# Up and down products of a gated MLP by seven half-block products each, with the samples apart and the gated values through DRAM

## The reference

```python
D_MODEL = 1024; SEQ = 1024; DEC_BATCH = 8; DEC_SEQ = 4; D_FF = 2816; FFN_CONV = 3
x = x + concat(heads) @ w_out                    # 1024 -> 1024
h = rmsnorm(x, ffn_norm_g)
up = h @ w_up                                    # 1024 -> 2 x 2816 (gate | value)
up, new_ffn = causal_dwconv(up, state, ffn_conv_w, ffn_conv_b)   # width 3, per column
gate, value = split(up)
y = x + (silu(gate) * value) @ w_down            # 2816 -> 1024
```

## Time and profile before

| what | value |
| --- | --- |
| median of 3 runs | 1661.88 us (1655.47 to 1668.57) |
| span of the profiled execution | 1659.6 us |
| TensorE busy | 1562.1 us, 94% |
| weight loads busy | 1477.7 us, 89% |
| VectorE busy | 996.4 us, 60% |
| ScalarE busy | 523.2 us, 32% |
| GpSimd busy | 307.1 us, 19% |
| bytes moved | 113.57 MB |

### The profile page before, as it was taken

One profiled execution on the slowest core, in us unless ns is written; L12 is line 12 of the kernel. 1 busy time (PEld: TensorE's weight loads), 2 busy tenths in 40 slices (PEclk: granted clock), 3 DMA queues, 4 the chain that ended last, 5 costly groups with the idle time before them and its releaser, 6 DMA issues.

```text
span 1659.6 us, 29004 instructions
## 1 busy us (share of the span) xinstructions
PE 1562.1 (94%) x11165; PEld 1477.7 (89%) x11165; DVE 996.4 (60%) x1507; ACT 523.2 (32%) x828; POOL 307.1 (19%) x698
## 2 busy tenths in 40 slices
PE   7999999997788888788999999999999999999998
PEld 7999999897577776455999999999999999999997
DVE  7444399786566666466445655646555565555654
ACT  6443333332344343444223221212212122121223
POOL 4000166563422342350000000000000000000000
PEclk8999999998799999899999999999999999999999
DMA  6211111222113110566212211102111021110104
GB/s 228 91 38 51 41 40 39 86 93 89 37 36 96 48 38 23 171 246 220 59 41 77 64 50 39 51 25 63 41 48 51 25 63 32 56 51 25 51 1 114
DMA packets 146857, 113.57 MB, mean 68 GB/s; under 512 B 21563, under 2 KB 134733, under 8 KB 145094
## 3 DMA queue, kind: packets, MB, share of 16 engines
q1 hardware_dynamic: 142456, 102.97, 21.0%
q0 software_dynamic: 1664, 6.29, 1.0%
q10 hardware_dynamic: 2656, 3.21, 0.5%
HBM read 90.59 MB, written 21.74 MB: 68 GB/s over the span
## 4 chain that ended last, share of the span: by engine, by line
PE 52%; DVE 1%; ACT 0%; DMA 0%; issue 0%; SPq 0%; DVEq 0%
PE f_up L3065 30%; PE f_down L3072 15%; PE f_up L193 4%; PE f_up L3025 1%; PE f_up L3052 1%; PE f_up L3072 0%; PE f_up L3110 0%; DMA f_rows<-in_ffn_conv_b 0%; PE f_up L3099 0%; PE f_down L3014 0%; ACT f_tail_tok L2827 0%; DVE dn_lo L2990 0%; PE f_down L3046 0%; DVE feat L2859 0%; DVE h_lo L2872 0%
## 5 line engine op out<-in xcount | busy, mean ns | idle before, releaser
L3065 PE MATMUL f_up<-h_hi,w_hi 128*128 128x352 f32 x1032 | 334.9, 324 | 0.0
L3065 PE MATMUL f_up<-h_hi,w_lo 128*128 128x352 f32 x1032 | 333.4, 323 | 0.0
L3065 PE MATMUL f_up<-h_lo,w_hi 128*128 128x352 f32 x1032 | 333.4, 323 | 0.0
L193 PE MATMUL proj<-x_hi,win_hi 128*128 128x352 f32 x672 | 219.9, 327 | 0.0
L193 PE MATMUL proj<-x_hi,win_lo 128*128 128x352 f32 x672 | 217.1, 323 | 0.0
L193 PE MATMUL proj<-x_lo,win_hi 128*128 128x352 f32 x672 | 216.9, 323 | 0.0
L3065 PEld LDWEIGHTS f_up<-h_hi,w_lo 128*128 128x128 f32 x1032 | 194.1, 188 | 0.0
L3065 PEld LDWEIGHTS f_up<-h_hi,w_hi 128*128 128x128 f32 x1032 | 193.8, 188 | 0.0
L3065 PEld LDWEIGHTS f_up<-h_lo,w_hi 128*128 128x128 f32 x1032 | 193.8, 188 | 0.0
L2949 DVE TENSOR_TENSOR feat<-f_down,feat 128x352 f32<-128x352 f32 x256 | 127.5, 522 | 65.2 <-PE f_down L3072 65.2
L3072 PE MATMUL f_down<-f_g_hi,dn_hi 128*128 128x352 f32 x512 | 165.3, 323 | 0.0
(11 more groups left out here) (464 smaller groups left out, 2799.4 us busy)
## 6 DMA issues: line engine op xcount, KB each, us to landing
w_raw<-in_w_up SPq DMA_DIRECT2D x44, 512.0 KB, 3.8
win_raw<-in_w_in SPq DMA_DIRECT2D x28, 512.0 KB, 4.1
dn_raw<-in_w_down SPq DMA_DIRECT2D x11, 1024.0 KB, 5.2
p_key<-in_cache_k SPq DMA_DIRECT2D x32, 256.0 KB, 3.6
x_scratch<-feat SPq DMA_DIRECT2D x1, 4224.0 KB, 12.0
feat<-x_scratch SPq DMA_DIRECT2D x8, 528.0 KB, 7.0
feat<-in_x_prompt SPq DMA_DIRECT2D x8, 512.0 KB, 8.0
c_DD<-dd_scratch SPq DMA_DIRECT2D x8, 512.0 KB, 4.0
```

What stands on the lines that cost most here:

```text
L193: mm = nc.tensor.matmul(out, w[:, k, :], x[:, k, g * TG:(g + 1) * TG], start=(k == 0 and i == 0), stop=(k == KT - 1 and i == 2))
L3065: mm = nc.tensor.matmul(up[u % RING][:, 0:TG], a[s][:, kk, :], b, start=(kk + x == 0), stop=(kk == KT - 1 and x == 2))
```

## The change

The samples leave the 1056 columns, so that the prompt is a square of two halves of 512 tokens. The up product of a pair (gate tile and value tile, 2 x 128 features, against 2 x 512 of the model's features and 2 x 512 tokens) is a 2 x 2 block product, made with seven products and fifteen sums instead of eight products. The names are P1 to P7. P1 to P4 and P6 have weights A11, A12, S4, A22 and S2, P5 and P7 have S1 and S3 (`W_OF`). The four weight sums S1 to S4 (`weight_sums`) are GpSimd's, 128x512 each, in each pair. The operand's sums are made once, before the first pair, and lie in SBUF with their high and low halves for all 22 pairs. A product is 4 x 3 matmuls of 512 columns, so a pair has 84. P1 is left in its bank and P2 is added on top of it, P7 and P4 on top of P6, P3 on top of P5; in between, copies are kept (`keep_u1` on ScalarE, the other six on VectorE), and the last of them write `f_pre`. The scaling by the root, which was part of L2915, is GpSimd's for three of the four quarters (`scale`). The high half of each weight tile is a ScalarE copy of 128x512 (`up_high`), the low half VectorE's (`up_low`), in a ring of five.

The gated values (1024 tokens) go to DRAM (`g_scratch`), and so does the residual (`h_scratch`). When all pairs are through, the down product runs in chunks of 3, 4 and 4 units of 256 features, by the same seven products: here each unit needs three token sums, three feature sums and two second ones on GpSimd (in chunk 0 the token sums are VectorE's), a high and a low half of both operands for each product (`b_high`, `b_low`), and results are added to `dn_C` in SBUF (`b_keep`). The residual comes back in chunk 1 (`add_h`). The 32 sample columns have products of their own on TensorE in plain fp32, in four column strips at a time: `few_up` (8 matmuls of 256 columns), `few_fold` (2) and `few_down` (4) for each pair.

```diff
+    h_scratch = nc.dram_tensor("h_scratch", (P, KT, SEQ), F32, kind="Internal").ap()
+    g_scratch = nc.dram_tensor("g_scratch", (FT, P, SEQ), F32, kind="Internal").ap()
...
+    OF = {"P1": PX, "P2": PX, "P6": PY, "P7": PY, "P4": PY, "P5": PZ, "P3": PZ}
+    FIRST_IN = ("P1", "P6", "P5")
+    LAST_IN = ("P2", "P4", "P3")
+    ORDER = ["P1", "P6", "P2", "P7", "P5", "P4", "P3"]
+    ORDER0 = ["P1", "P5", "P6", "P2", "P7", "P4", "P3"]
...
+    A11, A12, A21, A22 = quad(0, 0), quad(0, 1), quad(1, 0), quad(1, 1)
+    S1, S2, S3, S4 = (sums[:, s, :, :] for s in range(4))
+    W_OF = {"P1": A11, "P2": A12, "P3": S4, "P4": A22, "P5": S1, "P6": S2, "P7": S3}
+    S_NTH = {"P7": 1, "P6": 2, "P5": 3, "P3": 4}
...
+    CHUNKS = [(0, 3), (3, 4), (7, 4)]
...
+            def load_up(p):
+                if p == 0:
+                    sp.wait_ge(split_lo, done(NO - 1))
+                else:
+                    sp.wait_ge(sums_made, 4 * p)
+                    sp.wait_ge(up_lo, turn(p - 1, "P4") + 1)
+                    sp.wait_ge(few_done, p)
+                for s in range(2):
+                    sp.dma_start(up_raw[:, s, :, :], w_u[:, :, p * P + s * FF:(p + 1) * P + s * FF]).then_inc(up_in, 16)
...
+            def weight_sums(p):
+                pool.wait_ge(up_in, 32 * (p + 1))
+                if p == 0:
+                    pool.wait_ge(unit_done, FIRST - NG)
+                else:
+                    pool.wait_ge(up_lo, NP * p)
+                nc.gpsimd.tensor_tensor(S3, A11, A21, sub).then_inc(sums_made, 1)
+                pool.wait_ge(sums_made, 4 * p + 1)
+                nc.gpsimd.tensor_tensor(S2, A22, S3, sub).then_inc(sums_made, 1)
+                pool.wait_ge(sums_made, 4 * p + 2)
+                nc.gpsimd.tensor_tensor(S1, A21, A22, add).then_inc(sums_made, 1)
...
+            def scale(p, s, half, nth, count):
+                pool.wait_ge(kept, count)
+                if p == 0:
+                    pool.wait_ge(rstd_put, 3)
+                x = pre[s][:, F_PAD + half * HT:F_PAD + (half + 1) * HT]
+                nc.gpsimd.tensor_tensor(x, x, rstd[:, half * HT:(half + 1) * HT], mult).then_inc(scaled, 1)
...
+            for p in range(FT):
+                if p:
+                    scale(p - 1, 0, 1, 3, 6 * p)
+                    keep_tail(p - 1, 0)
+                put_state(p, 1)
+                put_state(p, 0)
+                if p + 1 < FT:
+                    weight_sums(p + 1)
+                scale(p, 1, 1, 1, 6 * p + 4)
+                scale(p, 1, 0, 2, 6 * p + 5)
+                keep_tail(p, 1)
+            scale(FT - 1, 0, 1, 3, 6 * FT)
...
+            def token_sums(k, u):
...
+                pool.wait_ge(b_lo, seq(k - 1, "P5", CHUNKS[k - 1][1] - 1) + 1)
+                nc.gpsimd.tensor_tensor(n["e"][1][:, u, :], n["d"][1][:, u, :], n["g"][1][:, u, :], sub).then_inc(b_t, 1)
+                pool.wait_ge(b_t, 3 * q + 1)
+                nc.gpsimd.tensor_tensor(n["g"][1][:, u, :], n["g"][1][:, u, :], n["a"][1][:, u, :], sub).then_inc(b_t, 1)
+                pool.wait_ge(b_t, 3 * q + 2)
+                pool.wait_ge(b_lo, seq(k, "P1", u) + 1)
+                nc.gpsimd.tensor_tensor(n["a"][1][:, u, :], n["e"][1][:, u, :], n["a"][1][:, u, :], add).then_inc(b_t, 1)
...
+            def feature_sums(k, u):
...
+                    pool.wait_ge(multiplied, NP * FT)
+                nc.gpsimd.tensor_tensor(n["e"][0][:, u, :], n["a"][0][:, u, :], n["g"][0][:, u, :], sub).then_inc(b_s, 1)
+                pool.wait_ge(b_s, 3 * q + 1)
+                pool.wait_ge(b_lo, seq(k, "P1", u) + 1)
+                nc.gpsimd.tensor_tensor(n["a"][0][:, u, :], n["d"][0][:, u, :], n["e"][0][:, u, :], sub).then_inc(b_s, 1)
...
+            def second_sums(k, u):
...
+                nc.gpsimd.tensor_tensor(n["b"][0][:, u, :], n["b"][0][:, u, :], n["a"][0][:, u, :], sub).then_inc(b_s4, 1)
+                pool.wait_ge(b_t, 3 * q + 3)
+                nc.gpsimd.tensor_tensor(n["b"][1][:, u, :], n["b"][1][:, u, :], n["a"][1][:, u, :], sub).then_inc(b_t4, 1)
...
+            def up_high(s):
...
+                else:
+                    act.wait_ge(multiplied, s - WR + 1)
...
+            def keep_u2(p):
+                dve.wait_ge(multiplied, turn(p, "P6") + 1)
+                dve.wait_ge(u1_kept, p + 1)
+                if p:
+                    dve.wait_ge(kept, 6 * p)
...
+            def keep_12(p):
+                dve.wait_ge(multiplied, turn(p, "P3") + 1)
+                dve.wait_ge(kept, 6 * p + 5)
+                plus(p, 6, part(0, 1), PZ[:, :], u2[:, :])
...
-            def add(it, d, bank):
-                dve.wait_ge(partial, ND * it + (d + 1))
-                h = hT[:, d // NG, (d % NG) * TG:(d % NG + 1) * TG]
-                nc.vector.tensor_tensor(h, bank[:, 0:TG], h, ALU.add).then_inc(summed, 1)
...
+            def b_low(k, name, u):
+                r = seq(k, name, u)
+                dve.wait_ge(b_hi, r + 1)
+                w, g = b_operands(k, name)
+                nc.vector.tensor_tensor(bw[r % RING_B][1][:, 0, :], w[:, u, :], r32(bw[r % RING_B][0][:, 0, :]), sub)
+                nc.vector.tensor_tensor(bg[r % RING_B][1][:, 0, :], g[:, u, :], r32(bg[r % RING_B][0][:, 0, :]), sub).then_inc(b_lo, 1)
...
+            def b_keep(k, name, f):
...
+                if name == "P1":
+                    dve.wait_ge(b_kept, kept_b(k - 1, "P3", f))
+                    nc.vector.tensor_tensor(C[:, f, two], src[:, :], C[:, f, two], add)
+                    x = C[:, HK + f, :].rearrange("p (x t) -> p x t", x=2)
+                    nc.vector.tensor_tensor(x, over(src[:, :], 1, [P, 2, HT]), x, add).then_inc(b_kept, 1)
+                    return
...
+            def add_h(x):
...
+                dve.wait_ge(b_kept, kept_b(1, "P2" if half == 0 else "P6", t) if t < HK else kept_b(1, "P4" if half == 0 else "P5", t - HK))
+                h = C[:, t, half * HT:(half + 1) * HT]
+                nc.vector.tensor_tensor(h, h, h_in[x % 2][:, :], add).then_inc(h_added, 1)
...
+            def product(p, name):
+                s = turn(p, name)
+                pe.wait_ge(up_lo, s + 1)
...
+                if name == "P2":
+                    pe.wait_ge(u1_kept, p + 1)
+                if name == "P7":
+                    pe.wait_ge(kept, 6 * p + 1)
...
+                (w_h, w_l), (x_h, x_l) = wop[s % WR], xop[name]
+                for j in range(HK):
+                    if p == 0:
+                        pe.wait_ge(x_lo_done[name], j + 1)
+                    for x, (a, b) in enumerate(((w_h, x_h), (w_h, x_l), (w_l, x_h))):
+                        mm = nc.tensor.matmul(OF[name][:, :], a[:, j, :], b[:, j, :], start=(name in FIRST_IN and j + x == 0),
+                                              stop=(name in LAST_IN and j == HK - 1 and x == 2), skip_group_check=True)
+                mm.then_inc(multiplied, 1)
...
+            def few_up(p):
...
+                for half in range(2):
+                    for j in range(4):
+                        k = 4 * half + j
+                        mm = nc.tensor.matmul(FEW[j * NS:(j + 1) * NS, 0:2 * P], x_few[:, k, :], up_raw[:, :, k, :],
+                                              start=(half == 0), stop=(half == 1))
...
+            def few_fold(p):
...
+                for s in range(2):
+                    mm = nc.tensor.matmul(FEW[:, (8 + s) * NS:(9 + s) * NS], few_sb[:, s * P:(s + 1) * P], fold[:, :], start=True, stop=True)
...
+            def few_down(p):
...
+                for j in range(4):
+                    mm = nc.tensor.matmul(YS[j * NS:(j + 1) * NS, 0:2 * P], prod[:, SEQ:T], wd_few[:, j * 2 * P:(j + 1) * 2 * P],
+                                          start=False, stop=(p == FT - 1))
...
+            def b_product(k, name, units=None):
...
+                    pe.wait_ge(b_lo, r + 1)
...
+                            b_free(k, name, f)
+                        for x, (a, b) in enumerate(((w_h, g_h), (w_h, g_l), (w_l, g_h))):
+                            mm = nc.tensor.matmul(B_OF[name][f][:, :], a[:, 0, f * P:(f + 1) * P], b[:, 0, :],
+                                                  start=(name in FIRST_IN and u + x == 0), stop=(name in LAST_IN and u == n - 1 and x == 2), skip_group_check=True)
```

1199 lines of the change are left out of this document (831 added, 368 removed).

## The result

The changed kernel takes 1734.8 us (median; 1732.2 to 1741.4) against 1660.7 before, ratio 1.0456 with an interval of 1.0414 to 1.0497: 4.6% slower, outside the forecast range. The profiled execution has a span of 1732.5 us.

The account below looks back on a forecast made before the run. It took the kernel before as TensorE-bound, the changed one as held by VectorE and GpSimd taking turns: 872.3 + 34.3 + 462.0 + 2 + 279.4 + 11 + 8 = 1669.0 us of span, stated as 1670, range 1598 to 1715.

Parts of the forecast that it names:

- longer loop: Rival for the up pairs: couples cost 2.0 us or the weight loop takes 23.5 us; 1702 us, bracket 1685 to 1730, chance 0.25.
- The pair's length: Steady up pair: two loops of nearly equal length, 21.7 and 21.6 us, taken as 22.0 us a pair.
- A pair's own work: TensorE's work in an up pair: 84 matmuls at 0.227 us plus 1.34 us for samples, 20.4 us.
- The two loops: In an up pair: P7 waiting 1.3 us for keep_u2 (21.7 us), and the loop through the weights (21.6 us).
- the loop of the load: In an up pair: weight load, GpSimd sums and scalings, first tap, cast, low halves and taps, 21.6 us.
- 872.3: End of the output projection in us, taken from the kernel before as the start of the sum.
- The first pair: Pair 0 of the up part: operand sums and casts while TensorE stands, 34.3 us, bounds 28 and 40.
- The down part: Three down chunks: 209.7 us of work plus waits for low halves, sums and keeps, 279.5 us, bounds 230 and 300.
- VectorE beside GpSimd: Operations reading two SBUF operands exclude each other, 1.68 us a couple of 512 columns; operations out of PSUM aren't held up.
- The clock: Granted clock halves after idle gaps on TensorE; four or five such gaps counted, +8 us.
- The second rival: Up pairs: couples cost 2.0 us or the weight loop takes 23.5 us instead of 22.0; 1702 us, chance 0.25.
- 22.4 us a pair: Up pair length from which the longer loop decides for slower, 1678.5 us being 1% over; slower had chance 0.34.

Follow-up runs that it names:

- e1: Changed kernel with the gate of the pair before moved ahead of the low half for the next pair's P1 on VectorE: 1698.1 us.
- e4: Changed kernel with GpSimd's four weight sums over 4 columns instead of 512 from pair 1 on, order and waits kept: 1697.2 us.
- e3: Changed kernel with the sample matmuls (few_up, few_fold, few_down) left out in the middle pairs, all waits kept: 1735.4 us.
- e5: Changed kernel with the order edits of e1 and e2, and the sample matmuls left out in the middle pairs: 1653.0 us.
- e6: Changed kernel, everything computed, with e1, e2, keep_u2 ahead of two taps, and some loads and ScalarE sample copies moved earlier: 1670.3 us.
- e2: Changed kernel with the store of a finished residual tile issued ahead of the next weight load on SyncE in the output projection: 1729.5 us.
- e12: e6 with down chunks 1 and 2's token sums on VectorE, pair 0's put_few earlier, the last eight residual additions among chunk 2's low halves: 1657.8 us.
- e9: Changed kernel with GpSimd's sums in down chunks 1 and 2 over 4 columns instead of 512, except one unit's four: 1703.1 us.

## Why the prediction was wrong

The 1734.8 us lie above the range (1715), beyond which the forecast left a chance of 0.10, and above the bracket of its longer loop (1730).

- **The pair's length** is the step that failed. "P7 waits for keep_u2 and would start at 8.17" and "I take 22.0": it is 24.3. The list of loops lacked the one through TensorE's own queue: few_down sits between P5 and P4 and waits for the gate of the pair before, and the gate sits on VectorE behind a low half whose weights are in flight. e1 and e4 each took 37 us off, e4 by shortening the gate alone. few_down isn't even needed for it: without it (e3) P4 waits some 2.7 us for keep_u3, which stands behind the same low half and gate. The rows were there to see it: the order of VectorE shows the gate behind the low half of up_raw, and I had the load landing 6 us after its issue.
- **A pair's own work**, "1.34 us a pair" for the samples, is 2.43, of which e5 found 2.0 in the time. I had read the four loads of the earlier trace rows as four strips; a plain fp32 matmul leaves two rows (x16 for 8 matmuls of few_up), so the price was per half matmul. The wide matmul at 227 ns is 229.5, 0.2 us a pair. Together 20.4 becomes 21.7.
- **The two loops** that I worked out were real but shorter than the rest: P7's wait is 0.58 us (1.3 forecast), and the loop of the load never ended last (e1: 22.60 us, where e6, without the wait, takes 21.73; so the wait costs 0.87, of which 0.58 is idle).
- **"872.3"**: I took the output projection as unchanged. Its loads stand on SyncE behind casts that wait on ScalarE for stores that stand on SyncE behind the loads; the projection takes 108.2 us where the kernel before takes 98.0, and e2 took 10.5 off. A queue that gains eight stores was never walked through.
- **The first pair**: 48.2 instead of 34.3. Its waits (3.8, 4.1, 7.0) are before P1, few_fold and few_up of pair 1; I had placed none before few_up. e12 brings the last to 2.0, and another takes its place.
- **The down part** was right in sum (279.5 and 279.0), in part by luck: the waits that I added up are 69.7 us and came to 48.9 (the first 12.5 and 5.3), and matmuls at half the clock, some 13 us, dearer ones at the full clock and slow starts behind waits filled the rest. In cause it was right: a wait of 5.3 us before P1 of chunk 1 (6.8 forecast) and 9.3 before P1 of chunk 2 (10.8), each for keeps behind low halves, and e9 shows that 40 us of the part come with GpSimd's sums. The prices differ by place: the 7.5 us for the copy of the sample result in P6 had been given to gate and token sums.
- **VectorE beside GpSimd** was right: the mutual exclusion of operations with two SBUF operands (gate 2.31 against 1.21, low halves 1.09 against 0.68), and none for operands in PSUM. This agrees with the Trainium skill, page "SBUF — State Buffer", section "SBUF: two separate sides", on the shared port pair. The rule of the Trainium skill's page "TensorE: Matmul & The Clock Gate", section "Wait — 56ns, not 53.3ns?", N/2.4 plus 2.5 ns, gives 215.8 ns for 512 columns and 109.2 for 256; 229.5 and 120 were measured, so for these fp32r matmuls the measurement decides.
- **The clock**: behind the eight longest waits of the down part (3.1 to 9.3 us) 5 to 11 matmuls each start 0.43 us apart, 512/1.2 GHz, 65 in all, some 13 us. As forecast in kind, but the forecast had 8 us for the whole and four or five gaps. Behind few_down's waits it fell too, once in this profile (a wait of 2.1 us).

The second rival (the loop is longer, 1702 us) had the sign and not the mechanism. What the forecast said for slower, 22.4 us a pair, was passed by 2 us.

The pairs of the runs with the gate behind the low half differ between profiles mostly by how often the clock falls behind few_down's wait: one pair in the changed kernel, three in e2 and five in e9 take 26.0 to 26.5 us. What stays open: why the clock falls behind one such wait and not behind another (1.67 us in e9 with a fall, 1.68 in the changed kernel without), and how the down part's 40 us divide. No run took GpSimd out of both the up and the down part at once.

## What to carry to other kernels

A product with fewer multiplications pays only if the sums have an engine of their own: here the 128 us less of wide matmuls (4752 at 160.8 ns, 2772 at 229.5) went into 53 us of sample matmuls (22 x 2.43), 40 us that GpSimd's sums bring to the down part, 37 us for one gate, 10 in the output projection, and other waits. Before pricing a loop, go down each in-order queue and ask of every waiting instruction what stands behind it that another engine needs; a gate behind a low half behind a load cost 37 us and one moved line took them back. And when an edit that removes work changes nothing (e3), look for the wait that grew in its place, and for the clock behind it, before calling the work free.

## What the runs showed of the hardware

A GpSimd operation over 4 columns instead of 512 shortens VectorE's operations with two SBUF inputs next to it (gate 2.31 to 1.21 us) and leaves those that read PSUM at 0.68. A matmul's time over its columns at the full clock is 13.3, 14.1 and 16.2 ns for 256, 352 and 512 columns. Four column strips of plain fp32 matmuls with 256 columns, two a strip, take 1.00 us and cost the wide matmuls around them another 0.2.
